# Attention output projection: from fp32 products to three rounded passes, split into a left half among the units and a right half behind them, with GpSimd making the low parts

## The chip, the cores and the metric

The kernel runs on one core of a Trainium2 chip. The metric is device time in microseconds for one inference step, the median of three runs: 1342.69 us (1341.06 to 1346.56). Smaller is better. The profile is one execution taken by the hardware profiler; its times are in microseconds from the first instruction.

## What is computed

Two layers over 512 prompt rows and 32 sample rows of width 1024. Layer 0 mixes tokens by pooling, layer 1 by band attention with 16 heads of 64; each is followed by a mixture of experts (32 experts, each row uses two) whose weights, 6 MB an expert, are read from HBM. The change is in layer 1, between the attention and the router:

```python
o = band_attention(q, band(k), band(v), qpos, kpos, rel_bias)   # softmax(q k / 8 + bias) v
y = jnp.einsum('bse,ed->bsd', o.reshape(B, S, D), w_o)          # the output projection, 1024 x 1024
...
xp = xp + yp                                                   # residual
xp = xp + hier_moe(rms_norm(xp, norm_ffn[i]), *moe_args)        # router, then experts
```

## The kernel before

Instructions are written out per engine, in a fixed order, with semaphores between them; there is no scheduler. The rows are held in four prompt tiles of 128 rows (0 to 3) and one of 32 sample rows.

**Units.** Attention runs as 36 units: for each prompt tile, from tile 3 down to tile 0, eight units of two heads (`PAIRS` = 8; 512, 384, 256 and 128 keys for tiles 3, 2, 1, 0), then four units for the sample rows. `t` counts them. `LONG_UNITS` = 16 are those of tiles 3 and 2. Each engine walks the same loop over `t`, one step behind the other:

- TensorE: `scores(t)` (L2353), transposes of the weights of unit t-2 (L2377), `values(t-3)` (L2393), then, in some steps, four products of the output projection (L2443).
- VectorE: `biased(t)` adds the bias (L1770), `scaled(t-1)` divides by the sum (a reciprocal L1779 and two tensor_scalar L1782), `pT_out(t-2)` copies the second head's transposed weights (L1790).
- ScalarE: `weights(t)` is the exponential (L1253), `pT_out(t-2)` copies the first head's transposed weights (L1264). After four units `oT_out` (L1277) copies the attention's output, transposed, to `oT`.
- GpSimd: `load_bias(u)` issues the load of unit u's bias (L882), once VectorE is done with unit u-5; `hide_later_chunk(u-1)` (L889) waits for the landing of the one before and masks a corner.

**The output projection** of a tile is 16 products (8 row blocks `k` of `w_o` times two column halves `hf`), each a 128x128 by 128x512 matmul in fp32, accumulated in one PSUM bank (`WO_BANK`). `products_at(t)` puts four of them, as one chunk, behind every second unit from t = 12 to 34, and behind each of t = 35 to 38 (tile 0). When a half is whole, VectorE adds it to the residual (`add_product`, L1798), and ScalarE squares a finished row early (`early_squares`, L1289). So rows of tiles 3, 2 and 1 are normalised and stored while the last units still run. The sample's projection (`sample_product`, L2421; 16 products of 32 columns, four side by side on TensorE, and a `fold`, L2428) comes behind the loop, and then `route(1)`: transposes (L1864), router logits (L1930), top-1 and top-2 on VectorE, and the first gather of rows.

**Three rounded passes** are in the kernel already, for the q, k, v projection: an operand is split into a rounded high part and the rest, both in fp32r, and `split_product` forms high·high + low·high + high·low:

```python
mm(out, x_hi, w_h, start=start, stop=False)
mm(out, x_lo, w_h, start=False, stop=False)
return mm(out, x_hi, w_l, start=False, stop=stop)
```

**Weight loads.** SyncE issues the experts' weights (gate, up and down, 2 MB each) into three sets of buffers. Those of the first three experts of layer 1 go into memory that the attention still uses, so each waits for its piece to come free: down of expert 1 and 2 and gate of expert 0 during the units, up and down of expert 0 when all attention output is out, gate and up of expert 1 when the sample's projection is done, gate of expert 2 at the router's logits, and up of expert 2 after the first gather (L621). Behind it the loads of expert 3 follow, freed piece by piece by the first expert's matmuls (L665).

## Time and profile before

| | before |
|---|---|
| median of 3 runs (lowest, highest) | 1342.69 us (1341.06, 1346.56) |
| profiled execution, first to last instruction | 1340.0 us; its own time is not listed apart, the median is 2.7 us above this span |
| TensorE busy | 1291.8 us (96%) |
| VectorE, ScalarE, GpSimd busy | 574.1, 304.7, 127.9 us |
| bytes moved | 459.65 MB, 343 GB/s over the span |
| attention units of layer 1 | from 700 to 840 us |
| router of layer 1 | from 840 to 875 us |
| experts of layer 1 | from 875 us to the end |

A row of instructions gives start, duration, engine, line, operation, output and inputs, and how often it comes in the merged row; in square brackets is how long the engine had been idle, and whose signal ended that. PE is TensorE's matmul, PEld its weight load, DVE VectorE, ACT ScalarE, POOL GpSimd, SPq SyncE's DMA queue. One fp32 matmul of the program stands as two MATMUL rows or counts.

### The profile page before, as it was taken

The page shows a single profiled execution, that of the slowest core. Times are in us where ns is not written, and L with a number is a line of the kernel's source. Part 1 is how long each engine was busy: PE and PEld are TensorE (multiplying, and loading weights), DVE is VectorE, ACT ScalarE, POOL GpSimd, SP SyncE. Part 2 cuts the span into 40 slices and gives each one's busy share as a digit, 9 for nine tenths or more (in the row PEclk, how much of TensorE's full clock was granted, in tenths as well). Part 3 has the DMA queues.
Part 4 walks back from the last instruction along what each step waited for, and adds up shares of the span by engine and source line. Part 5 has one row for each costly group of instructions (what it writes and reads, how often), then busy time and mean ns, then how long its engine had stood idle before and what let it go on. Part 6 is the DMA issues. An engine that isn't in the chain of part 4 may idle for free.

```text
span 1340.0 us, 19743 instructions
## 1 busy us (share of the span) xinstructions
PE 1291.8 (96%) x7448; PEld 638.2 (48%) x7448; DVE 574.1 (43%) x1062; ACT 304.7 (23%) x650; POOL 127.9 (10%) x205
## 2 busy tenths in 40 slices
PE   8899999999999999999999999899999999999998
PEld 6643344333343334788777544443444334343333
DVE  4543334433333433864419543543334334343433
ACT  4211111111111113443436432211111111111111
POOL 2010000000000000232233210000000000000000
PEclk9989999999999999999999999899999999999999
DMA  9989999999999999222058512999999999999996
GB/s 360 380 334 420 424 428 426 427 429 427 428 427 427 428 425 402 69 93 97 34 174 273 181 33 78 380 344 420 426 427 426 427 428 428 427 428 427 426 426 255
DMA packets 53569, 459.65 MB, mean 343 GB/s; under 512 B 8141, under 2 KB 9421, under 8 KB 28170
## 3 DMA queue, kind: packets, MB, share of 16 engines
q1 hardware_dynamic: 41246, 426.48, 76.5%
q0 software_dynamic: 9616, 23.95, 5.5%
q10 hardware_dynamic: 2652, 8.45, 1.7%
q8 instruction: 39, 0.64, 0.2%
q14 instruction: 16, 0.13, 0.0%
HBM read 455.44 MB, written 11.26 MB: 348 GB/s over the span
## 4 chain that ended last, share of the span: by engine, by line
PE 91%; issue 3%; DVE 3%; ACT 2%; DMA 1%; POOL 0%; SPq 0%; DVEq 0%; ACTq 0%; POOLq 0%
PE ps L2014 34%; PE ps L2045 11%; PE ps L2023 9%; PE ps L2024 8%; PE ps L2443 4%; PE ps L1843 3%; PE ps L1845 3%; PE ps L1844 3%; PE ps L2006 2%; PE ps L2377 1%; PE ps L2393 1%; PE ps L1916 1%; PE ps L2032 1%; PE ps L2353 1%; PE ps L1864 1%
## 5 line engine op out<-in xcount | busy, mean ns | idle before, releaser
L1592 DVE TENSOR_TENSOR x<-x,ps 128x1024 f32<-128x1024 f32 (+1 forms) x150 | 177.7, 1216 | 220.9 <-PE ps L2045 219.8
L1606 DVE SCALAR_TENSOR_TENSOR nat<-nat,slot_gate,ps 64x256 f32<-64x256 f32 x128 | 86.1, 672 | 196.3 <-ACT nat L1093 164.7
L2014 PE MATMUL ps<-pair,xT 128*64 128x512 f32 x352 | 163.8, 616 | 6.1 <-issue 6.1
L2014 PE MATMUL ps<-ring,xT 128*64 128x512 f32 x352 | 160.9, 606 | 8.0 <-issue 6.4
L2015 PE MATMUL ps<-pair,xT 128*64 128x512 f32 x352 | 164.0, 616 | 0.0
L2045 PE MATMUL ps<-y_parts,hot 64*128 64x512 f32 (+1 forms) x1200 | 161.3, 403 | 0.0
L2015 PE MATMUL ps<-ring,xT 128*64 128x512 f32 x352 | 161.1, 607 | 0.0
L2014 PE MATMUL ps<-third_pair,xT 128*64 128x512 f32 x320 | 143.6, 596 | 6.9 <-issue 6.9
L1093 ACT ACTIVATE nat<-ps 64x512 f32<-64x512 f32 x62 | 36.8, 594 | 485.5 <-PE ps L2015 485.5
L2024 PE MATMUL ps<-qk,hidT 128*64 128x512 f32 x320 | 144.9, 595 | 0.0
L2023 PE MATMUL ps<-qk,hidT 128*64 128x512 f32 x320 | 144.8, 595 | 0.0
L2015 PE MATMUL ps<-third_pair,xT 128*64 128x512 f32 x320 | 143.8, 597 | 0.0
L2045 PEld LDWEIGHTS ps<-y_parts,hot 64*128 64x128 f32 (+1 forms) x1200 | 98.9, 171 | 72.3 <-issue 48.7
L1569 DVE TENSOR_TENSOR y_parts<-ps,y_parts 128x512 fp32r<-128x512 f32 x60 | 41.5, 692 | 132.5 <-ACT y_parts L1078 132.5
L2014 PEld LDWEIGHTS ps<-pair,xT 128*64 128x64 f32 x352 | 46.9, 140 | 97.2 <-issue 96.0
L2014 PEld LDWEIGHTS ps<-ring,xT 128*64 128x64 f32 x352 | 46.3, 139 | 96.5 <-issue 95.5
L2014 PEld LDWEIGHTS ps<-third_pair,xT 128*64 128x64 f32 x320 | 41.4, 137 | 85.8 <-issue 84.7
L2023 PE MATMUL ps<-ring,hidT 128*64 128x512 f32 x176 | 79.6, 595 | 1.6 <-ACT xT L1059 1.6
L2024 PE MATMUL ps<-ring,hidT 128*64 128x512 f32 x176 | 79.7, 596 | 0.0
L1078 ACT ACTIVATE y_parts<-ps 128x512 fp32r<-128x512 f32 x60 | 35.8, 597 | 192.4 <-PE ps L2024 192.4
L1843 PE MATMUL ps<-w_hi,hT_hi 128*128 128x512 f32 x192 | 76.8, 400 | 0.7 <-DVE hT_lo L1374 0.7
L769 POOL DMA_INDIRECT nat<-xn,gcol x30 | 30.7, 1022 | 467.9 <-PE ps L2006 428.8
(261 smaller groups left out, 1780.3 us busy)
## 6 DMA issues: line engine op xcount, KB each, us to landing
qk<-in_moe_w_down SPq DMA_DIRECT2D x40, 2048.0 KB, 28.5
ring<-in_moe_w_down SPq DMA_DIRECT2D x22, 2048.0 KB
ring<-in_moe_w_gate SPq DMA_DIRECT2D x20, 2048.0 KB, 23.7
ring<-in_moe_w_up SPq DMA_DIRECT2D x20, 2048.0 KB
third_pair<-in_moe_w_gate SPq DMA_DIRECT2D x20, 2048.0 KB, 22.7
third_pair<-in_moe_w_up SPq DMA_DIRECT2D x20, 2048.0 KB
pair<-in_moe_w_gate SPq DMA_DIRECT2D x18, 2048.0 KB
pair<-in_moe_w_up SPq DMA_DIRECT2D x18, 2048.0 KB, 29.7
```

Source lines behind the costliest of these rows:

```text
L1569: V.tensor_tensor(y_rest[v], ps[:, bank, :], f32(y_high[v]), ALU.subtract).then_inc(y_lo[l], 1)
L1592: return V.tensor_tensor(x[0:n, i, :], x[0:n, i, :], ps[0:n, bank:bank + 2, :].rearrange("p b c -> p (b c)"), ALU.add)
L1606: last = V.scalar_tensor_tensor(out=out[u * BLK:(u + 1) * BLK, :].rearrange("s (k p) -> s k p", k=n), in0=act_rows[:, u * n:(u + 1) * n, : ...
L1843: mm(out, x_hi, w_h, start=start, stop=False)
L1844: mm(out, x_lo, w_h, start=False, stop=False)
L1845: return mm(out, x_hi, w_l, start=False, stop=stop)
L2014: mm(ps[BLK:P, GU_BANK, :], rows, gate[:, at], start=(k == 0), stop=(k == KT - 1))
L2015: last = mm(ps[0:BLK, GU_BANK, :], rows, up[:, at], start=(k == 0), stop=(k == KT - 1))
L2023: mm(ps[0:BLK, bank, :], rows, slot[:, at:at + 512], start=(k == 0), stop=(k == FT - 1))
L2024: last = mm(ps[BLK:P, bank, :], rows, slot[:, at + 512:at + D], start=(k == 0), stop=(k == FT - 1))
L2045: last = mm(ps[0:n, bank + hf, :], (hot[v] if by is None else by)[slots, tok(i)], part[slots, :], start=first and at == 0, stop=final and ...
L2443: last = mm(ps[:, WO_BANK, :], oT[:, k, tok(i)], wo_all[:, k, hf * 512:(hf + 1) * 512], start=(k == 0), stop=(k == KT - 1))
```

## The change

The output projection is done with `split_product` on rounded parts. The 16 blocks of `w_o` (c = 0 to 15; 8 of the left half, 8 of the right) are loaded apart, 256 KB each: the first eight into `pair`, the others into places of `nat` and `qk` as tiles finish. ScalarE rounds the high part of each block (`wo_rounded`) and of each group of attention output (`oT_rounded`); GpSimd subtracts to make the low parts (`wo_rest`, `oT_rest`, 25 tensor_tensor instructions on 128x512 elements, the last on 128x256) between its bias loads. The left half of tiles 3, 2 and 1 runs one product behind each of t = 15 to 22 and 25 to 32 and two behind each of t = 34 to 37. Behind the loop stand tile 0's left half, the sample's left half, and then the whole right half. Squares, scaling and stores of the finished rows move behind the loop. From unit 16 on VectorE no longer copies transposed weights: one ScalarE instruction copies both heads' (`pT_both`). The load of down for expert 1 moves behind the projection.

```diff
+        PRODUCTS = {**{15 + k: [(TILES - 1, k)] for k in range(KT)}, **{25 + k: [(TILES - 2, k)] for k in range(KT)},
+                    **{34 + k // 2: [(TILES - 3, k - 1), (TILES - 3, k)] for k in range(1, KT, 2)}}
+        ADDED_AT = {max(t for t, at in PRODUCTS.items() if at[0][0] == i): i for i in range(1, TILES)}
+        WO_SPLIT = {**{6 + c: c for c in range(8)}, **{21 + c - 8: c for c in range(8, 14)}, 31: 14, 38: 15}
...
             def pT_out(t):
+                elif t < PROMPT_UNITS:
+
+                    act.wait_ge(pT_ps, heads_through(t))
+                    act.activation(pT_both[t % 2][:, :, 0:n], ps[:, PT_BANK:PT_BANK + 2, 0:n], ACT.Copy).then_inc(pT_first, 1)
...
+            def wo_rounded(c):
+
+                s, count = wo_landed(c)
+                act.wait_ge(piece_in[s], count)
+                act.activation(wo_part(c, 1), wo_raw(c), ACT.Copy).then_inc(split_hi, 1)
...
+            def wo_rest(c):
+
+                pool.wait_ge(split_hi, QKV_QUARTERS + c + 1)
+                last_own(split_lo, QKV_QUARTERS + c + 1)
+                pool.tensor_tensor(wo_part(c, 0), wo_raw(c), f32(wo_part(c, 1)),
+                                   ALU.subtract).then_inc(split_lo, 1)
...
             for u in range(BIASES, PAIRS * TILES):
                 load_bias(u)
                 if u > BIASES:
                     hide_later_chunk(u - 1)
+                rests(u - BIASES)
...
-            def tile_product(i, first, n):
...
-                    last = mm(ps[:, WO_BANK, :], oT[:, k, tok(i)], wo_all[:, k, hf * 512:(hf + 1) * 512],
-                              start=(k == 0), stop=(k == KT - 1))
...
+            def part_product(hf, i, k):
+
+                c = hf * KT + k
+                pe.wait_ge(split_lo, QKV_QUARTERS + c + 1)
+                return split_product(ps[:, WO_BANKS[hf][i], :], oT_hi[:, k, tok(i)], oT_lo[:, i, k, :],
+                                     wo_part(c, 1), wo_part(c, 0), k == 0, k == KT - 1)
...
-                if products_at(t) is not None:
-                    tile_product(*products_at(t))
+                for i, k in PRODUCTS.get(t, []):
+                    if k == 0:
+                        pe.wait_ge(oT_lo_sb, GROUPS_OUT * (TILES - i) // TILES)
+                        if i < TILES - 1:
+                            pe.wait_ge(x_half, turn(3, i))
+                    last = part_product(0, i, k)
+                    if k == KT - 1:
+                        last.then_inc(att_y, 1)
+
+            pe.wait_ge(oT_lo_sb, GROUPS_OUT)
+            for k in range(KT):
+                last = part_product(0, 0, k)
+            last.then_inc(att_y, 1)
+            pe.wait_ge(oT_lo_sb, GROUPS_OUT + 1)
+            for k in range(KT):
+                last = sample_product(0, k)
+            last.then_inc(quarters_used, 1)
+            for i in range(TILES - 1, -1, -1):
+                if i == 0:
+                    pe.wait_ge(x_half, TILES)
+                    for k in range(KT):
+                        last = sample_product(1, k)
+                    last.then_inc(stack_ps, 1)
+                for k in range(KT):
+                    last = part_product(1, i, k)
+                last.then_inc(att_y, 1)
             transposes(3, TILES - 1)
-            for hf in range(2):
-                sample_product(hf)
             route(1)
```

How TensorE's row of instructions looks among the units of tile 0 (128 keys), before: two units, and a chunk of four products ahead of them and behind them. L2443 is a product, L2353 scores, L2377 transposes, L2393 values.

```order
L2443 MATMUL ps<-pair,third_pair 128x512 x4
L2353 MATMUL ps<-qk 128x128 x2
L2377 MATMUL ps<-cst,gain 128x128 x2
L2393 MATMUL ps<-ring,nat 64x128 x2
L2353 MATMUL ps<-qk 128x128 x2
L2377 MATMUL ps<-cst,ring 128x128 x2
L2393 MATMUL ps<-ring,nat 64x128 x2
L2443 MATMUL ps<-pair,third_pair 128x512 x4
```

The same place now, where scores are L2475, transposes L2499, values L2515 and a product's three passes L1965 to L1967:

```order
L1965 MATMUL ps<-wo_pair,oT_hi 128x512
L1966 MATMUL ps<-wo_pair,oT_lo 128x512
L1967 MATMUL ps<-wo_pair,oT_hi 128x512
L2475 MATMUL ps<-qk 128x128 x2
L2499 MATMUL ps<-cst,ring 128x128 x2
```

One product instead of four, but behind every unit; between two units stand three short matmuls.

GpSimd's queue at units 11 to 14 before: a bias load is issued, and the mask of the one before is set when that has landed (`bias_in`).

```order
L882 DMA ring<-in_rel_bias_reversed 128x2x384 [waits s_biased]
L889 MEMSET ring 64x2x64 [waits bias_in0]
L882 DMA ring<-in_rel_bias_reversed 128x2x384 [waits s_biased]
L889 MEMSET ring 64x2x64 [waits bias_in1]
L882 DMA gain<-in_rel_bias_reversed 128x2x384 [waits s_biased]
L889 MEMSET ring 64x2x64 [waits bias_in2]
```

The same queue now (the load is L935, the mask L951, `wo_rest` L985, `oT_rest` L978):

```order
L951 MEMSET ring 64x2x64 [waits bias_ready,bias_in1]
L985 TENSOR_TENSOR wo_pair<-pair,wo_pair 128x512 [waits bias_ready,split_hi]
L935 DMA gain<-in_rel_bias_reversed 128x2x384 [waits s_biased]
L951 MEMSET ring 64x2x64 [waits split_lo,bias_in2]
L985 TENSOR_TENSOR wo_pair<-pair,wo_pair 128x512 [waits bias_ready,split_hi]
L935 DMA ffn_gain<-in_rel_bias_reversed 128x2x384 [waits s_biased]
L951 MEMSET gain 64x2x64 [waits split_lo,bias_in3]
L978 TENSOR_TENSOR oT_lo<-third_pair,oT_hi 128x512 [waits bias_ready,oT_sb]
L985 TENSOR_TENSOR wo_pair<-pair,wo_pair 128x512 [waits oT_lo_sb,split_hi]
```

A subtraction or two now stand between a mask and the next unit's load. Behind the loop TensorE's queue was, from the last values on:

```order
L2409 MATMUL ps<-ring,nat 64x32 x2
L2443 MATMUL ps<-pair,third_pair 128x512 x4
L1864 MATMUL ps<-cst,x 128x128 x8
L2421 MATMUL ps<-pair,third_pair 32x512 x16
L1864 MATMUL ps<-cst,x 128x128 x8
L2428 MATMUL ps<-gain,cst 32x512 x2
L1864 MATMUL ps<-cst,x 128x128 x16
L1930 MATMUL ps<-third_pair,rw 64x384 x8
```

Now 24 passes for tile 0's left half, 16 for the sample's (L2549 to L2552), 72 for the right half of tiles 3, 2 and 1, 16 more for the sample and 24 for tile 0 stand there, and then:

```order
L1967 MATMUL ps<-wo_nat,oT_hi 128x512
L1986 MATMUL ps<-cst,x 128x128 x16
L2557 MATMUL ps<-gain,cst 32x512 x2
L1986 MATMUL ps<-cst,x 128x128 x16
L2052 MATMUL ps<-third_pair,rw 64x384 x8
```

The transposes, the fold and the router's logits keep their order; 40 products, 24 of them of tiles 3 to 1, have moved in front of them from the loop.

## Rows read from the trace of the kernel before

**Rows 1.** Windows: busy us and (count) per engine, granted clock, DMA share, GB/s.

```profile
core 0: us, PE busy (x) PEld busy (x) DVE busy (x) ACT busy (x) POOL busy (x), PEclk, DMA share, GB/s
...
782.00:837.00 55.00, 53.02 (x331) 26.83 (x330) 20.63 (x100) 19.24 (x74) 3.88 (x9) 1.00 0.19 58
...
850.00:875.00 25.00, 21.01 (x90) 11.68 (x90) 15.99 (x55) 4.48 (x11) 1.98 (x2) 0.80 0.83 339
...
900.00:1150.00 250.00, 249.59 (x1450) 101.31 (x1448) 98.94 (x135) 36.45 (x73) 10.80 (x18) 1.00 1.01 426
1150.00:1300.00 150.00, 140.61 (x794) 57.15 (x792) 54.88 (x75) 19.77 (x40) 4.80 (x8) 0.98 1.01 427
```

**Rows 2.** SyncE's DMA queue, timeline around the start of layer 1's experts.

```profile
872.35 0.33 SPq L621 DMA_DIRECT2D third_pair<-in_moe_w_up  x1
877.02 0.33 SPq L665 DMA_DIRECT2D ring<-in_moe_w_gate  x1
```

**Rows 3.** The chain that ended last, from the last chunk to the logits: start, us, what.

```profile
836.67 3.63 PE ps L2443 x8
...
841.19 3.62 PE ps L2421 x32
...
847.77 0.69 DVE x L1798
848.48 1.16 ACT xT L928 x2
...
850.49 2.80 PE ps L1930 x16
```

**Rows 4.** TensorE, timeline: a chunk of four products, and what starts behind it.

```profile
761.94 3.70 PE L2443 MATMUL ps<-pair,third_pair 128*128 128x512 f32 x8
765.57 0.70 PE L2353 MATMUL ps<-qk 64*128 64x256 f32 x4
...
836.60 3.70 PE L2443 MATMUL ps<-pair,third_pair 128*128 128x512 f32 x8
...
840.13 1.05 PE L1864 MATMUL ps<-cst,x 128*128 128x128 f32 x8
```

**Rows 5.** TensorE, timeline in the q, k, v projection: three rounded passes.

```profile
689.63 0.39 PE L1843 MATMUL ps<-w_hi,hT_hi 128*128 128x512 f32 x1
...
690.31 0.39 PE L1843 MATMUL ps<-w_hi,hT_hi 128*128 128x512 f32 x1
```

**Rows 6.** TensorE, groups by line in 733 to 837 us: busy, mean ns, idle before.

```profile
L2377 PE MATMUL ps<-cst,ring 128*128 128x128 f32 x76 | 12.8, 285 | 3.4 <-ACT ring L1264 2.4 <-DVE ring L1790 0.9
```

**Rows 7.** Timeline of unit 11: VectorE's work, and TensorE's transposes that wait.

```profile
732.40 0.56 DVE L1770 CUSTOM_DVE_ANT_0 ring<-ps,ring 128x384 f32<-128x384 f32 x1 [0.31 <-issue]
...
733.56 0.75 DVE L1782 TENSOR_SCALAR ring<-ring 128x384 f32<-128x384 f32 x2
734.23 0.55 DVE L1790 COPY ring<-ps 128x384 f32<-128x384 f32 x1
734.87 0.56 DVE L1770 CUSTOM_DVE_ANT_0 ring<-ps,ring 128x384 f32<-128x384 f32 x1
...
734.88 0.30 PE L2377 MATMUL ps<-cst,ring 128*128 128x128 f32 x1 [0.15 <-ACT ring L1264]
```

**Rows 8.** A line's instructions: duration ns min/median/max, first and last start, forms.

```profile
L860 POOL TENSOR_TENSOR nat<-nat,qk_gain x20: 1275/1298/2278, 560.5 to 657.6; 128x512 f32<-128x512 f32 x16, 32x512 f32<-32x512 f32 x4
...
L1361 DVE TENSOR_TENSOR w_lo<-ring,w_hi x24: 1210/1226/2307, 534.3 to 677.3; 128x1024 fp32r<-128x1024 f32 x24
```

**Rows 9.** Timeline around 562 us: a subtraction on VectorE beside a product on GpSimd.

```profile
561.75 2.28 POOL L860 TENSOR_TENSOR nat<-nat,qk_gain 128x512 f32<-128x512 f32 x1
...
562.80 2.31 DVE L1361 TENSOR_TENSOR w_lo<-ring,w_hi 128x1024 fp32r<-128x1024 f32 x1
```

**Rows 10.** Timeline of GpSimd's bias loads and masks, and VectorE's scaling beside one.

```profile
722.80 0.72 POOL L882 DMA_DIRECT2D ring<-in_rel_bias_reversed  x1
...
724.82 0.91 DVE L1782 TENSOR_SCALAR ring<-ring 128x512 f32<-128x512 f32 x2
...
725.11 0.33 POOL L889 MEMSET ring<- 64x128 f32 x1 [1.60 <-DMA ring<-in_rel_bias_reversed]
...
727.30 0.20 POOL L889 MEMSET ring<- 64x128 f32 x1 [1.21 <-DMA ring<-in_rel_bias_reversed]
```

More of the change, by code:

```diff
@@ L290, in encoder, with wo_part, wo_raw @@
         rw_experts = xT_flat[:, KT * NG:KT * NR].rearrange("p (g n) -> p g n", g=NG)
+        pair_flat = pair[:, :, :].rearrange("p a n -> p (a n)")
+        def wo_part(c, part):
+            where, u = WO_PLACES[c]
+            return wo_parts[where][:, u, part, :]
+        def wo_raw(c):
+            where, u = WO_PLACES[c]
+            flat = (pair_flat, nat[:, :], qk_flat[:, SLOT:])[where]
+            return flat[:, u * 1024:u * 1024 + 512]
         early_rows = third_pair[:, 1, :]
@@ L305, in encoder @@
                  for u in range(2)]
+        pT_both = [a4[:, 2 * D + u * 1024:2 * D + (u + 1) * 1024].rearrange("p (h n) -> p h n", h=2) for u in range(2)]
         BIASES_RING, BIASES = 3, 5
@@ L910, in _ @@
                     hide_later_chunk(u - 1)
+                rests(u - BIASES)
             hide_later_chunk(PAIRS * TILES - 1)
+            for t in range(PAIRS * TILES - BIASES, UNITS + 4):
+                rests(t)
+            oT_rest(GROUPS_OUT)
             experts(1)
@@ L1013, in logitsT_out @@
                 act.wait_ge(logitsT_ps, 2 * l + part + 1)
-                cols = part_cols(part)
+                cols = part_cols(part) if part == 0 else slice(part_cols(part).start, NT * P)
                 act.activation(logitsT[:, cols], ps[:, LOGITST_BANKS[l][part], 0:cols.stop - cols.start],
@@ L1292, in _ @@
             for t in range(UNITS + 4):
-                if t >= 4 and t - 4 < PROMPT_UNITS and (t - 4) % OT_GROUP == OT_GROUP - 1:
-                    oT_out(t - 4)
+                if group_at(t, OT_GROUP + 3) is not None:
+                    oT_out(group_at(t, OT_GROUP + 3))
                 if t < UNITS:
@@ L1300, in _ @@
                     pT_out(t - 2)
-                for i, hf in halves_before(t - 1):
-                    if hf == 1 and i > 0:
-                        early_squares(i)
+                if group_at(t, OT_GROUP + 4) is not None:
+                    oT_rounded(group_at(t, OT_GROUP + 4))
+                if t in WO_SPLIT:
+                    wo_rounded(WO_SPLIT[t])
                 if t == UNITS:
                     load_sqrt_table()
-                    act.wait_ge(act_own, own[0])
-                    act.activation(std[:, 3, 1:TILES], ssq[:, 3, 1:TILES], ACT.Sqrt, bias=const("eps"),
-                                   scale=1.0 / D).then_inc(std_ready, TILES - 1)
-            oT_out(UNITS - 1)
+            oT_out(GROUPS_OUT)
+            oT_rounded(GROUPS_OUT)
             for i in range(TILES - 1, 0, -1):
+                early_squares(i)
+            act.wait_ge(act_own, own[0])
+            act.activation(std[:, 3, 1:TILES], ssq[:, 3, 1:TILES], ACT.Sqrt, bias=const("eps"),
+                           scale=1.0 / D).then_inc(std_ready, TILES - 1)
+            for hf in range(2):
+                wo_stack_out(hf)
+            for i in range(TILES - 1, 1, -1):
                 store_row(1, i)
@@ L2411, in values @@
                 last.then_inc(o_ps, 1)
-            def sample_product(hf):
-                if hf == 0:
-                    pe.wait_ge(oT_sb, OT_ALL)
-                    pe.wait_ge(x_mixed[1], TILES)
-                half = slice(hf * 512, (hf + 1) * 512)
-                for k in range(KT):
-                    at = k % HEADS_A_GROUP * SS
-                    last = mm(ps[at:at + SS, WO_SAMPLE_BANKS[hf], :], oT[:, k, S:T], wo_all[:, k, half],
-                              start=(k < HEADS_A_GROUP), stop=(k >= KT - HEADS_A_GROUP))
-                last.then_inc(stack_ps, 1)
+            def part_product(hf, i, k):
[3 more added lines that the diff above has]
+                                     wo_part(c, 1), wo_part(c, 0), k == 0, k == KT - 1)
@@ L2425, in sample_fold @@
             def sample_fold(hf):
                 pe.wait_ge(stack_sb, 2 * QKV_PIECES + hf + 1)
[L2428 removed]
+                mm(ps[0:SS, WO_SAMPLE_BANKS[hf], :], const("fold", 2 * SS), wo_stacked[hf], start=True,
                    stop=True).then_inc(att_y, 1)
[L2431 to L2446 removed]
```

214 lines of the change are left out of this document (136 added, 78 removed).

## The prediction

> **What bounds the kernel now.** I read the windows by stage first. From 900 us to the end of the experts the DMA engines are busy all the time at 426 to 427 GB/s [rows 1], while in the attention (782 to 837 us) their share is 0.19 and in the router it is 0.83. So the experts' stage is a stream of fixed length, and what counts is when it starts. It starts where the first experts' buffers, all filled ahead, begin to come free: SyncE's queue issues the last of the nine early loads at 872.35, and expert 3's first piece at 877.02, when the first expert's matmuls free it [rows 2]. Both hang on the router. Loads that the change delays (down of expert 1, gate and up of expert 1) land long before that, in a stage whose DMA is mostly idle; they cost nothing as long as 2 MB at that rate, 5 us, fit between the end of the projection and the first gather, some 30 us later.
>
> Then the chain of waits, from the attention to the router. It is on TensorE: the last chunk, the sample's products, then short steps on VectorE and ScalarE, and the logits at 850.49 [rows 3]. TensorE is busy for 53.02 of 55 us in the last units [rows 1]; its own waits for the pipeline from 733 to 837 us are 3.4 us before the transposes of the weights [rows 6]. So up to the logits the time is TensorE's queue, and an edit is worth what it takes out of it or makes it wait. From the logits on the program is as before; I carry a shift there through to the end.
>
> **The sum.** I count up to the end of the last values (836.6) and from there to the logits.
>
> *Removed before 836.6.* A chunk of four fp32 products moves what follows by 765.57 - 761.94 = 3.63 us [rows 4]. Fifteen of the sixteen lie there (t = 12 to 34 by twos, 35, 36, 37): 54.5 us.
>
> *Added before 836.6.* Three rounded passes take 690.31 - 689.63 = 0.68 us, 0.227 each [rows 5], against 0.91 for a product of a chunk. But a chunk has a cost of its own when the next matmul is of another shape. In the chunk at 836.60 the same eight matmuls take 3.53 us [rows 4], so that 0.10 depends on the neighbour; the rows of a chunk are some 0.43 apart, 3.42 in all, by which the cost is 0.1 to 0.2. I take 0.21, since the new chunks stand between values and scores as that of 761.94 does. Sixteen chunks of one product make 16 x 0.89 = 14.2 us, four of two make 4 x 1.57 = 6.3, together 20.5.
>
> *Behind 836.6.* Before, the logits come 13.9 us later: 3.5 for the last chunk, 3.6 for the sample [rows 3], and 6.8 for transposes, fold, two additions, a square of the sample's rows and a copy. Now 40 products (27.2) and 32 passes for the sample (7.3) come first, 34.5 us, and the same 6.8 behind them: 41.3. The additions, squares and scalings of tiles 3 and 2 lie beside the 34.5 us; of tile 1, one scaling on VectorE comes behind the last product, beside TensorE's transposes and fold. Net 27.4 us more.
>
> These three give 54.5 - 20.5 - 27.4 = 6.6 us less.
>
> *The pipeline's waits.* The chunks of 3.63 us behind every second unit let VectorE and ScalarE run ahead. With 0.89 behind every unit, TensorE still has more to do in a unit than the round trip takes in most units; units 23, 24, 32 and 33 have no product and will wait some tenths each. VectorE gains its copy (0.55 us [rows 7]) in units 16 to 31, ScalarE gets some 0.5 us a unit more and was busy for only 19.24 of 55 us [rows 1]. Bounds: 1.4 and 6 us against 3.4 before. I take 2.4, so 1.0 less.
>
> *GpSimd's subtractions.* No such instruction stands in the attention now; the nearest row is the product of 128x512 on GpSimd, 1.29 us undisturbed and up to 2.28 [rows 8]. Two that meet say why [rows 9]: while GpSimd runs, VectorE's subtraction of two SBUF operands goes from 1.23 to 2.31, and GpSimd's from 1.29 to 2.28; each waits for the other's whole instruction. What stands beside them in the attention is VectorE's tensor_scalar, with one SBUF operand. The only row for it is the mask of 725.11, which took 0.33 instead of 0.20 beside a tensor_scalar of 724.82, while that was not slowed [rows 10]: they do meet, by 0.13 at least. Upper bound: a full block. In units 7 to 15 VectorE is busy for 2.38 of 2.47 us and TensorE's transposes start right when its copy ends [rows 7], so there a delay of VectorE is one of TensorE. A subtraction that starts at any time in 2.47 us holds up the first of the two tensor_scalars for 0.65 us on average in 1.29/2.47 of the cases, and comes between the two, for the whole 1.29, in 0.34/2.47 (0.34 being about half of their 0.75): 0.51 us, less 0.09 of slack. Ten subtractions fall there (blocks 0 to 7, groups 0 and 1): 4.2 us. Thirteen come in later units, where VectorE has 0.8 us to spare without its copy: 0.1 each, 1.3. So between 0 and 5.5; I take 3.0, the middle, as the row nearest in place shows a part of the block and the row nearest in kind all of it.
>
> *Low parts that come late.* GpSimd waits for a bias to land, 4.5 us after its issue (722.80 to 727.30 [rows 10]), before each mask; with a subtraction of 1.29 behind the mask a step takes (4.5 + 0.2 + 1.3)/2 = 3.0 us instead of 2.47, over eight units some 4 us of lag. The masks are made four units ahead and stay in time. The low part of tile 3 is made two units, 5 us, ahead of its first product, behind such a lag: 0 to 2 us late; by then TensorE has lost some of the same time, so 0.5. Queued behind GpSimd's waits are only its own masks; behind TensorE's wait are all scores that follow.
>
> Sum: -6.6 - 1.0 + 3.0 + 0.5 = -4.1. The span goes from 1340.0 to 1335.9, and with the 2.7 us between span and median the time is **1338.6 us**. With its own bounds that case reaches from 1336 to 1341.
>
> **The rule on the shared port.** The rows above show full blocking for two SBUF operands, and a small one for a tensor_scalar. The Trainium skill says in "SBUF — State Buffer", section "Who interferes with whom", that tensor_scalar can run in a mode that takes the port pair VectorE shares with GpSimd, and that the later of the two then "fully blocks" until the first is done. By that the block of 5.5 us above holds in full, the low parts come later too (1.0), and the sum is -6.6 - 1.0 + 6.5 = -1.1: 1341.6. No row here shows it for a tensor_scalar beside a GpSimd instruction that reads. That speaks against this change, and has a chance of its own below.
>
> **Rivals.**
> *GpSimd costs little.* If a tensor_scalar isn't held up and the low parts are in time, the sum is -7.6, and with chunks that cost 0.10 like that of 836.60 instead of 0.21 another 20 x 0.1 = 2.0 less: -9.6, 1333.1. For it: tensor_scalar of 724.82 kept its 0.91 beside the mask. Against: the full blocking of [rows 9].
> *Full block:* 1341.6, worked out above.
> *The two engines lock into step.* Low parts start when masks end, not at random; if each of the 23 subtractions comes just ahead of or between the tensor_scalars, each costs up to 1.29 less the slack: 10 x 1.20 + 13 x 0.49 = 18.4. Then -7.6 + 18.4 + 0.5 = +11.3, 1354.0, slower. It decides from 14.3 us of GpSimd's cost on (that gives +6.7). Against it: bias landings vary from step to step.
> *It is hidden behind DMA.* If the weight stream, not the router, set the restart, nothing would move: 1342.7. For it: the share of 1.01 [rows 1]. Against: at 850 to 875 us the share is 0.83, and expert 3's first load waits for matmuls, not for room in the queue.
>
> **Chances and range.** The forecast's case 0.37, GpSimd costs little 0.31, full block 0.15, locked into step 0.10, hidden 0.07. A measurement of this kernel can tell 0.5% (6.7 us, below 1336.0 or above 1349.4) from no change. Faster: all of the second case and a sixth of the first, 0.37. Slower: the step-lock and a few hundredths of the unforeseen, 0.13. Within: 0.50. The range reaches from the cheap case, 1332, to beyond the full block, 1346; it leaves out the step-lock and the low end of the second case, about 2 in 10.
>
> **What would show it right or wrong.** In the profile after: passes 0.227 us apart among the units and behind them; the logits some 41 us behind the last values, and at about 846.4 instead of 850.5; last values near 805 instead of 836.6; GpSimd's subtractions at 1.3 us, or up to 2.3 where they meet; VectorE's tensor_scalar longer than its 0.75 for two in units 7 to 15, which decides between the cases; TensorE's waits before the transposes at 2 to 9 us; the wait for the low part before the first product of tile 3 under 2 us; the DMA share still 1.01 from 900 us on. The prediction is wrong if the logits' shift isn't the end's, if ScalarE's rounding delays the exponentials (TensorE would wait for ScalarE's copies in each unit), or if the clock that is granted in the router (0.80 from 850 to 875 us [rows 1]) falls otherwise.

## The result: 0.3% slower, and the profile after

The changed kernel takes 1348.52 us (median of 20 executions, 1341.04 to 1354.26); the kernel before took 1343.76 beside it. The ratio is 1.0031, with a 95% interval from 1.0015 to 1.0046; one execution of the kernel before took 1626.41 us and is left out of it. That is some 4 us slower, where 4 us less were forecast, and outside the range. The profiled execution of the changed kernel spans 1344.3 us, 4.3 more than that of before.

Windows of the changed kernel (columns as in [rows 1]):

```profile
core 0: us, PE busy (x) PEld busy (x) DVE busy (x) ACT busy (x) POOL busy (x), PEclk, DMA share, GB/s
782.00:837.00 55.00, 52.07 (x345) 36.61 (x344) 13.22 (x60) 18.99 (x60) 13.99 (x15) 0.94 0.57 216
850.00:875.00 25.00, 22.11 (x101) 12.88 (x101) 15.30 (x47) 7.24 (x16) 1.39 (x2) 0.80 0.58 207
900.00:1150.00 250.00, 249.04 (x1450) 101.47 (x1448) 97.84 (x135) 37.03 (x75) 10.83 (x18) 1.00 1.01 426
```

The experts' stage is the same stream at 426 GB/s, and the router has the clock of before, 0.80. What is new is the 0.94 from 782 to 837 us, where before had 1.00.

TensorE, timeline: the first scores, a wait before the transposes of a unit, the last values, the logits.

```profile
703.06 2.00 PE L2475 MATMUL ps<-qk 64*128 64x256 f32 x16
...
737.91 0.85 PE L2499 MATMUL ps<-cst,ring 128*128 128x128 f32 x6 [1.44 <-issue]
...
813.27 0.30 PE L2531 MATMUL ps<-ring,nat 32*64 32x32 f32 x4
...
854.78 2.80 PE L2052 MATMUL ps<-third_pair,rw 128*64 128x384 f32 x16 [0.79 <-ACT third_pair L1092]
```

Before, the logits began at 850.49 [rows 3] and the span ended 489.5 us later; here it is 854.78 and again 489.5. So in these two profiles the shift of the logits is that of the end, and all of it arises before them. (Over all fourteen profiles that last part takes 488.3 to 492.6 us.) The attention itself began 3.1 us later (703.06; before 699.92), with the same instructions ahead of it; a control below shows what that is worth. To be rid of it I compare the stretch from the first scores to the logits: 150.6 us before, 151.7 now, forecast 146.5 (150.6 less 4.1).

From the last values to the logits it is 41.2 us (854.78 - 813.57), as forecast (41.3; before 13.9). The loss lies among the units: 110.5 us from the first scores to the last values, forecast 105.2. TensorE's waits there, 700 to 815 us:

```profile
PE ps L2499 <- issue: 4.7, 6, 1.4
PE ps L2515 <- ACT third_pair L1375: 2.7, 1, 2.7
```

The first line is the one that I had priced: units 7 to 15, where VectorE is late. The profile names no releaser for it; experiment 2 shows that these waits go with GpSimd's subtractions. The second is one wait that no step of mine had. Around it, ScalarE:

```profile
783.94 0.63 ACT L1391 ACTIVATE wo_nat<-nat 128x512 fp32r<-128x512 f32 x1 [2.52 <-DMA nat<-in_attn_w_o]
784.48 0.58 ACT L1375 ACTIVATE third_pair<-ps 128x512 f32<-128x512 f32 x1
```

SyncE's queue:

```profile
760.74 0.33 SPq L665 DMA_DIRECT2D nat<-in_attn_w_o  x1
...
780.79 0.33 SPq L665 DMA_DIRECT2D nat<-in_attn_w_o  x1
```

And TensorE:

```profile
785.20 0.70 PE L2515 MATMUL ps<-ring,nat 128*64 128x128 f32 x4 [2.69 <-ACT third_pair L1375]
...
788.75 0.70 PE L2515 MATMUL ps<-ring,nat 128*64 128x128 f32 x4
...
792.06 0.44 PE L2515 MATMUL ps<-ring,nat 128*64 128x128 f32 x4
792.43 0.50 PE L1965 MATMUL ps<-wo_pair,oT_hi 128*128 128x512 f32 x1
```

At unit 26's step ScalarE rounds block 13 of `w_o`. That block was issued at 760.74, but ScalarE waits until 783.94. The reason is in the code: `WO_LOADS` counts the landings of blocks 13 and 14 together, on one semaphore, and block 14 is issued only when tile 1's place in `nat` is free, at 780.79, in that same step. Behind the rounding stands `oT_out`, and for that TensorE's values wait 2.69 us. Then TensorE goes on slowly: a unit's step takes 3.55 us from 785.20 to 788.75. The windows of 2 us say why:

```profile
782.00:784.00 2.00, 0.50 (x4) 0.27 (x2) 1.19 (x8) 0.06 (x1) 1.03 (x3) 1.00 0.51 170
...
786.00:788.00 2.00, 2.00 (x7) 1.17 (x7) 0.00 (x0) 0.09 (x1) 1.80 (x4) 0.50 0.11 25
788.00:790.00 2.00, 2.00 (x10) 1.11 (x9) 1.07 (x7) 1.31 (x6) 0.88 (x2) 0.50 0.28 49
...
792.00:794.00 2.00, 2.00 (x15) 1.18 (x13) 1.01 (x8) 1.15 (x5) 0.70 (x1) 1.00 0.20 49
```

A granted clock of 0.50 is 1.2 GHz in place of 2.4. TensorE stood idle, and right behind it the clock was at half until shortly before 792.

### The profile page after: what moved, and what is told of

Read it like the earlier page. It is cut to its first block, busy times and chain, and to the rows that moved or that the text cites. A ratio compares the mean times of both kernels' runs of the same rounds, so it can differ in the third digit from the quotient of the medians.

```text
span 1344.3 us, 19958 instructions
## 1 busy us (share of the span) xinstructions
PE 1289.9 (96%) x7512; PEld 655.1 (49%) x7512; DVE 577.8 (43%) x1046; ACT 321.0 (24%) x675; POOL 158.7 (12%) x230
## 4 chain that ended last, share of the span: by engine, by line
PE 92%; issue 3%; DVE 2%; ACT 1%; DMA 1%; POOL 0%; SPq 0%; POOLq 0%; DVEq 0%; ACTq 0%
PE ps L2136 34%; PE ps L2167 11%; PE ps L2145 9%; PE ps L2146 8%; PE ps L1965 5%; PE ps L1967 4%; PE ps L1966 4%; PE ps L2128 2%; PE ps L2515 2%; PE ps L2499 2%; PE ps L2475 1%; PE ps L2038 1%; PE ps L2154 1%; PE ps L1961 1%; PE ps L2374 1%
## 5 line engine op out<-in xcount | busy, mean ns | idle before, releaser
L2136 PE MATMUL ps<-ring,xT 128*64 128x512 f32 x352 | 162.8, 612 | 9.8 <-issue 8.2
L2136 PE MATMUL ps<-pair,xT 128*64 128x512 f32 x352 | 160.6, 606 | 5.8 <-issue 5.8
L2137 PE MATMUL ps<-ring,xT 128*64 128x512 f32 x352 | 163.0, 613 | 0.0
L2137 PE MATMUL ps<-pair,xT 128*64 128x512 f32 x352 | 160.8, 607 | 0.0
L2136 PE MATMUL ps<-third_pair,xT 128*64 128x512 f32 x320 | 145.0, 601 | 6.7 <-issue 6.7
L2146 PE MATMUL ps<-qk,hidT 128*64 128x512 f32 x320 | 144.9, 595 | 0.0
L1965 PE MATMUL ps<-w_hi,hT_hi 128*128 128x512 f32 x192 | 77.4, 403 | 0.7 <-DVE hT_lo L1493 0.7
```

What stands on the lines that cost most here:

```text
L2136: mm(ps[BLK:P, GU_BANK, :], rows, gate[:, at], start=(k == 0), stop=(k == KT - 1))
L2137: last = mm(ps[0:BLK, GU_BANK, :], rows, up[:, at], start=(k == 0), stop=(k == KT - 1))
L2146: last = mm(ps[BLK:P, bank, :], rows, slot[:, at + 512:at + D], start=(k == 0), stop=(k == FT - 1))
```

## The experiments

**0. Control: the kernel before again.**

> The kernel before once more, as a control. In the profile after, the attention began at 703.06 us instead of 699.92, with the same instructions in front of it; 1.5 us of that come from layer 0 and 1.6 from a short fall of the granted clock near 560 us. Theory A (that offset of 3.1 us is chance and not the change's): this kernel's profile begins the attention anywhere in 699 to 704 us, its executions lie within some 1340 to 1349 us, with a mean granted clock of 0.983 to 0.987 in all of them. Theory B (the changed kernel is slower because TensorE's clock falls more often in it): the same for this kernel, but with a visibly narrower spread of the clock than the 0.975 to 0.986 of the changed one. If this kernel's executions show 0.975 to 0.980 too, B is out.

Measured: ratio 1.0017 (0.9999 to 1.0035); executions from 1341.62 to 1351.16 us, mean clock 0.980 to 0.988, both a little wider than I had allowed. Its profile has the first scores at 705.98, also later than allowed, and the stretch to the logits is 150.8 us, 0.2 more than in [rows 3]. The first scores of all fourteen profiles of this study lie between 699.7 and 706.0: the offset of 3.1 us is chance, and the stretch is what can be compared. Theory B isn't out: none of these 12 executions, and none of the 35 of the kernel before beside them, has a mean clock below 0.980, while 8 of the changed kernel's 20 have (0.975 to 0.979), and these 8 took 1348 us or more. The medians are 0.985 and 0.980.

**1. Block 13's landing counted alone.** One line of the changed kernel:

```diff
-        WO_LOADS = [(0, range(0, 4)), (1, range(4, 8)), (2, range(8, 13)), (0, range(13, 15)), (1, range(15, 16))]
+        WO_LOADS = [(0, range(0, 4)), (1, range(4, 8)), (2, range(8, 13)), (0, range(13, 14)), (1, range(14, 15)), (0, range(15, 16))]
```

> The changed kernel with one edit: the landing of block 13 of w_o is counted apart from that of block 14 (which is issued only at unit 26's step, just when ScalarE rounds block 13). Theory A: the wait of 2.52 us in front of ScalarE's rounding of block 13 is gone, with it TensorE's wait of 2.69 us before the values at 785, and the half clock that followed it (some 2 us): 4.7 us less than the changed kernel, 1343.8 against 1348.5. Theory B (the clock falls because of the many short waits in units 7 to 15): only the 2.7 us go, 1345.8, and the executions still spread over some 12 us with clocks down to 0.975.

Measured: 1337.66 us, ratio 0.9966 (0.9945 to 0.9987); median clock 0.987.

```profile
704.27 2.00 PE L2475 MATMUL ps<-qk 64*128 64x256 f32 x16
...
782.18 0.44 PE L2515 MATMUL ps<-ring,nat 128*64 128x128 f32 x4
...
784.25 0.44 PE L2515 MATMUL ps<-ring,nat 128*64 128x128 f32 x4
...
849.78 2.80 PE L2052 MATMUL ps<-third_pair,rw 128*64 128x384 f32 x16 [0.79 <-ACT third_pair L1092]
```

The wait is gone and a step takes 2.07 us. The stretch is 145.5 us, 6.2 less than in the changed kernel: the wait of 2.7, the half clock (two steps of 3.4 on average in place of 2.05, 2.7 in all), and 0.8 of other waits. The median fell by more than the 4.7 us that I expected, by 10.9 (8.7 by the ratios). So this one pair of counts makes a slower kernel out of a faster one. Theory B had the short waits of units 7 to 15 bring on the fall; they are still here, and the clock is 1.00 from 700 to 840 us. The executions do still spread over 10 us. That the median gains more than the profile shows fits the clock, by an estimate: 0.980 and 0.987 differ by 0.007 x 1345 = 9.4 us of full clock, more than the one fall of the profiled execution. Where the rest of it lies no profile shows.

**2. Ten subtractions cut to a sixteenth.**

```diff
+                    m = slice(0, 8) if g < 2 else slice(0, P)
+                    pool.tensor_tensor(oT_lo[:, i, at, m], oT_raw[:, i, at, m], f32(oT_hi[:, at, tok(i)])[:, :, m],
...
+                m = slice(0, 32) if c < 8 else slice(0, 512)
+                pool.tensor_tensor(wo_part(c, 0)[:, m], wo_raw(c)[:, m], f32(wo_part(c, 1))[:, m],
...
```

> The changed kernel with ten of GpSimd's subtractions (w_o blocks 0 to 7 and tile 3's two groups, all in units 7 to 15) cut to a sixteenth of their elements; the products read the high part in place of those low parts, so the output is not the reference's but every matmul is issued. Theory A (VectorE's tensor_scalar waits for the whole GpSimd instruction): the pairs of tensor_scalar that took 0.83 to 2.64 us go back to 0.75 to 0.8, TensorE's waits between 733 and 752 (4.4 us) go, 1344.1. Rival (the units are late because of the bias loads and masks behind GpSimd's longer queue, or ScalarE's added rounding): the tensor_scalars shorten but TensorE gains under 1.5 us, 1347. The wait at block 13 stays in both.

Measured: 1346.21 us, ratio 1.0026 (1.0006 to 1.0046), which by the time alone can't be told from the changed kernel's 1.0031. In the profile Theory A holds. TensorE's waits up to the last values fell from 9.3 to 4.5 us, but the stretch only from 151.7 to 150.2, since the clock stayed low longer behind the wait for block 14:

```profile
778.00:780.00 2.00, 2.00 (x9) 1.07 (x7) 0.00 (x0) 0.45 (x3) 1.81 (x4) 0.50 0.00 0
780.00:790.00 10.00, 10.00 (x39) 5.54 (x39) 3.32 (x21) 4.44 (x17) 3.78 (x4) 0.50 0.21 66
```

Some 13 us at half clock here, some 7 in the changed kernel's profile, behind the same wait of 2.7. The waits of units 7 to 15 don't bring the fall on: they are gone here, and the fall is not. Six of these 12 executions have a mean clock below 0.980.

**5. The wait filled with work.** In front of the values that wait in the changed kernel:

```diff
+                        if t == 24:
+                            for _ in range(6):
+                                mm(ps[:, S_BANK, 256:512], ident, some[:, 0:256], start=True, stop=True,
+                                   skip_group_check=True)
                         pe.wait_ge(oT_sb, 2 * (t // OT_GROUP) - 1)
```

> The changed kernel (block 13 still counted with block 14), with six matmuls of 128x256 on the identity, some 2.7 us of work, put in front of the values for which TensorE waits 2.69 us. The wait stays as long, but the engine is busy in it. Theory C (what costs most is not the wait but the half clock that the wait brings on behind it: 6.8 us of half clock in the changed kernel's profile, 13.6 in that of e2): the granted clock stays 1.00 from 780 to 800 us, 4 to 7 us less than the changed kernel (1348.5), so 1342 to 1344.5, and 3 to 4 us above e1. Rival (the half clock is brought on by the product chunks or the mix of short matmuls there): as the changed kernel, 1348.5.

Measured: 1341.24 us, ratio 0.9981 (0.9963 to 0.9999), 7.3 us less than the changed kernel by the medians, 6.7 by the ratios; none of the 12 executions has a mean clock below 0.982, and in the profile it is 1.00 from 780 to 800 us. Timeline of TensorE:

```profile
780.02 2.76 PE L2512 MATMUL ps<-cst 128*128 128x256 f32 x12
782.77 0.44 PE L2519 MATMUL ps<-ring,nat 128*64 128x128 f32 x4
```

The values are as late as without the filling, and the steps behind them take 2.05 us. So of the price of that wait one part, 2.4 us in the stretch (147.9 against experiment 1's 145.5), is the wait itself. The other part is the half clock behind it: the stretch is 3.8 us shorter than the changed kernel's, 1.1 of it in other waits, so 2.7, and the median gains more than that. The Trainium skill says in "TensorE: Matmul & The Clock Gate", section "Why this matters for your kernels", that a TensorE left idle between matmuls drops to its lower clock. By the changed kernel and this run that is so at this place. It is not so each time: in the changed kernel's own profile TensorE waits 2.65 and 2.66 us between two experts, with the same work before and behind, and only one of the two waits is followed by a fall.

```profile
1227.53 0.61 PE L2136 MATMUL ps<-pair,xT 128*64 128x512 f32 x1 [2.65 <-issue]
1288.36 0.61 PE L2136 MATMUL ps<-third_pair,xT 128*64 128x512 f32 x1 [2.66 <-issue]
```

The windows of 8 us behind them (the granted clock is the third figure from the end):

```profile
1228.00:1236.00 8.00, 8.00 (x38) 3.18 (x36) 2.35 (x2) 0.00 (x0) 0.00 (x0) 0.79 1.01 428
1289.00:1297.00 8.00, 8.00 (x45) 3.36 (x42) 2.35 (x2) 0.00 (x0) 0.00 (x0) 1.00 1.01 428
```

What decides between them no run here shows.

**6. Small subtractions, with block 13 counted alone** (edits of 1 and 2 together).

> e1 with the ten subtractions of units 7 to 15 cut to a sixteenth as in e2 (their products read the high part instead, so the output is not the reference's). This measures the blocks without the half clock on top. TensorE waited 3.3 us between 725 and 752 us in e1. Theory A: those waits go, from the first scores to the logits 142.5 us instead of 145.5, 1334.7. Rival (VectorE catches up later by itself, since TensorE has other waits to absorb it): under 1 us less than e1.

Measured: 1335.01 us, ratio 0.9948 (0.9934 to 0.9961); the stretch is 142.3 us. This is the price of the ten subtractions, 3.2 us, from one profile of each kernel; the ratios of experiments 1 and 6 overlap in their intervals. The view of a block in the changed kernel, two of VectorE's pairs of tensor_scalar in units 7 to 15:

```profile
734.70 2.64 DVE L1901 TENSOR_SCALAR ring<-ring 128x384 f32<-128x384 f32 x2
...
744.59 0.83 DVE L1901 TENSOR_SCALAR ring<-ring 128x384 f32<-128x384 f32 x2
```

GpSimd beside the first of them:

```profile
734.44 1.27 POOL L978 TENSOR_TENSOR oT_lo<-third_pair,oT_hi 128x512 fp32r<-128x512 f32 x1
735.86 1.26 POOL L985 TENSOR_TENSOR wo_pair<-pair,wo_pair 128x512 fp32r<-128x512 f32 x1
```

And VectorE in experiment 6:

```profile
733.97 0.75 DVE L1903 TENSOR_SCALAR ring<-ring 128x384 f32<-128x384 f32 x2
```

The pair that met two subtractions lost 1.89 us; GpSimd's instructions never took over 1.32. This is the full block of the rule in the Trainium skill, "SBUF — State Buffer", section "Who interferes with whom", seen here for a tensor_scalar: VectorE's instruction stands until GpSimd's has ended.

**3, 4 and 8. The splitting of `w_o` moved to where VectorE has room.**

```diff
-        WO_SPLIT = {**{6 + c: c for c in range(8)}, **{21 + c - 8: c for c in range(8, 14)}, 31: 14, 38: 15}
+        WO_SPLIT = {**{16 + c: c for c in range(14)}, 31: 14, 38: 15}
```

with the products later by some steps, as each expectation says, and in 4 and 8 in GpSimd's loop:

```diff
                 load_bias(u)
-                if u > BIASES:
-                    hide_later_chunk(u - 1)
                 rests(u - BIASES)
+                if u > BIASES + 1:
+                    hide_later_chunk(u - 2)
```

> e1's edit, and the splitting of w_o moved as a whole to steps 16 to 29, where VectorE no longer copies transposed weights; the left-half products follow (tile 3 at 19 to 26, tile 2 at 27 to 34, tile 1 two by two at 35 to 38). Nothing is left out. Theory A: the blocks cost next to nothing there (two tensor_scalars of 256 or 128 columns take 0.62 of a unit in which VectorE idles 0.7 to 1.2 us), the two groups of tile 3 still cost some 1 us: 3.4 us less than e1, 1340.4. Rival (there is no slack there either, TensorE loses 0.5 us for each block): as e1, 1343.8. Rival (low parts come late for the first products, three steps behind their splitting): slower than e1 by 2 us or more, with TensorE waiting for POOL.

> e3 with its own trouble mended: in e3 a mask on GpSimd waited 5.3 us for a bias load that shared the DMA queues with 2 MB of the gate weights, the low part of a w_o block stood behind it, and TensorE waited 4.3 us in front of a product. Here each mask is set one step later and the subtraction stands ahead of it, and tile 3's products follow at steps 20 to 27, tile 2's at 28 to 35, tile 1's by three, three and two at 36 to 38. Theory A (VectorE's tensor_scalar waits for GpSimd only where the unit has no slack): from the first scores to the logits 142.5 us (e1 145.5, e3 149.8), so 3 us less than e1, 1334.7. Rival (the blocks cost the same wherever they are): as e1, 1337.7. Rival (a low part is late again): over 1340, with a wait for POOL in TensorE's list.

> e4 lost 3.4 us in one wait at 782: tile 2's first product stood one step behind tile 3's last, in the same PSUM bank, and VectorE's addition that empties it was queued behind the next unit's work. Here one step lies between them (tile 3 at steps 19 to 26, tile 2 at 28 to 33, tile 1 at 35 to 38); masks later and late splits as in e4; and on ScalarE the copy of tile 1's last transposes goes ahead of the square of the sample's rows (0.8 us before the logits). Theory A: e4's 148.2 us from the first scores to the logits, less 3.4, less 1.7 of half clock, less 0.8: 142.3, three below e1's 145.5, 1334.5. Rival (late splits always trade the blocks for another wait): 145 or more, as e1 or slower.

Measured: 3 has 1343.08 us (ratio 1.0004, 0.9983 to 1.0025), a stretch of 149.8; 4 has 1344.4 (1.0007, 0.9993 to 1.0021), 148.2; 8 has 1338.04 (0.9963, 0.9942 to 0.9985), 144.9. In each the blocks of units 7 to 15 are gone (but for those of tile 3's two groups), and in each another wait has come. GpSimd's timeline in 3: the mask stands until the bias has landed, behind 2 MB of gate weights, and the subtraction behind the mask.

```profile
762.99 0.20 POOL L951 MEMSET gain<- 64x128 f32 x1 [5.26 <-DMA gain<-in_rel_bias_reversed]
763.34 1.26 POOL L985 TENSOR_TENSOR wo_pair<-pair,wo_pair 128x512 fp32r<-128x512 f32 x1
```

TensorE's in 3, then in 4:

```profile
764.65 0.76 PE L1965 MATMUL ps<-wo_pair,oT_hi 128*128 128x512 f32 x1 [4.33 <-POOL wo_pair L985]
```

```profile
782.34 0.47 PE L1966 MATMUL ps<-wo_pair,oT_hi 128*128 128x512 f32 x1 [3.37 <-issue]
```

The wait in 3 is the second rival of its expectation. The wait in 4 has two causes in a row. I placed tile 2 directly behind tile 3, in the bank that VectorE had yet to empty. And VectorE, whose addition empties it, was itself late: it had stood 2.95 us for a mask, which GpSimd set only behind two subtractions, in the order that this experiment's own edit made.

```profile
780.53 0.29 DVE L1890 CUSTOM_DVE_ANT_0 ring<-ps,gain 128x128 f32<-128x128 f32 x1 [2.95 <-POOL gain L951]
...
781.56 0.68 DVE L1918 TENSOR_TENSOR x<-x,ps 128x512 f32<-128x512 f32 x1
```

Behind both the granted clock was 0.83 over ten microseconds, where neighbours had 1.00. In 8 no wait is over 1.2 us, but they sum to 5.6 us as in experiment 1: 3 us of blocks were traded for waits on ScalarE (2.9 us), VectorE (1.2) and low parts (0.8). The rival of experiment 8 held: its stretch is experiment 1's within 0.6 us.

**7. Each tile product one fp32 matmul, in place.**

```diff
-                return split_product(ps[:, WO_BANKS[hf][i], :], oT_hi[:, k, tok(i)], oT_lo[:, i, k, :],
-                                     wo_part(c, 1), wo_part(c, 0), k == 0, k == KT - 1)
+                return mm(ps[:, WO_BANKS[hf][i], :], f32(oT_hi[:, k, tok(i)]), f32(wo_part(c, 1)),
+                          start=(k == 0), stop=(k == KT - 1))
```

> e1 with every product of the four prompt tiles as one fp32 matmul on the rounded high parts (low parts are made but not read by them, so the output is not the reference's); order, splitting, waits and the sample's product are e1's. This tells what the three passes give by themselves. By my sum a product costs 0.91 instead of 0.68 us: 64 x 0.23 = 14.7 us more than e1 from the first scores to the logits, 160.2 us, and 1352.4. Rival (in the units TensorE waits for VectorE in any case, so that 20 products among them hide a part of it): 10 to 12 us more, 1348 to 1350.

Measured: 1347.89 us, ratio 1.0042 (1.0026 to 1.0057), a stretch of 156.6, 11.1 us more than experiment 1. Nothing of it is hidden: behind the last values the 40 products take 7.1 us more, 0.18 each, and the 24 among the units 4.0, 0.17 each. So an fp32 product costs 0.68 + 0.18 = 0.86 us, which is what the forecast's chunk of 3.63 gives less its 0.21; my expectation of 14.7 had counted the chunk's own cost with each product. The 11.1 us lie in the rival's range, but its reason, that waits among the units hide a part, did not hold.

**9. The copies apart.**

```diff
-                if t < LONG_UNITS:
+                if t < PROMPT_UNITS:
                     act.wait_ge(pT_ps, heads_through(t - 1) + 1)
...
-                if 0 <= t - 2 < LONG_UNITS:
+                if 0 <= t - 2 < PROMPT_UNITS:
                     pT_out(t - 2)
...
```

> e1 with the third part of the change undone: in units 16 to 31 VectorE copies the second head's transposed weights again, ScalarE only the first's. By my sum VectorE's 0.5 us a unit there was worth 1.0 us of TensorE's waits together with everything else, so 0 to 2 us more than e1: 145.5 to 147.5 from the first scores to the logits. Rival (without that relief the pipeline is bound by VectorE in every unit, as in units 7 to 15): 16 x 0.3 = 5 us more, 150, with waits for VectorE's copy in each unit.

Measured: 1340.49 us, ratio 0.997 (0.9953 to 0.9987); stretch 147.3, 1.8 more than experiment 1. TensorE's waits for the pipeline are 7.5 in place of 5.6 us. So this part of the change is worth some 2 us by the profiles, within what I had expected; by the ratios experiments 1 and 9 are the same.

**10. Products in pairs behind every second unit.**

```diff
-        PRODUCTS = {**{15 + k: [(TILES - 1, k)] for k in range(KT)}, **{25 + k: [(TILES - 2, k)] for k in range(KT)},
+        PRODUCTS = {**{15 + k: [(TILES - 1, k), (TILES - 1, k + 1)] for k in range(0, KT, 2)},
+                    **{25 + k: [(TILES - 2, k), (TILES - 2, k + 1)] for k in range(0, KT, 2)},
```

> e1 with the products of tiles 3 and 2 two by two behind every second unit (steps 15, 17, 19, 21 and 25, 27, 29, 31) instead of one behind each. My sum gives each chunk 0.21 us of its own: 8 fewer chunks, 1.7 us less than e1, 143.8 us from the first scores to the logits, 1336. Rival (the cover that a chunk gives VectorE and ScalarE is then missing behind every other unit, and TensorE waits there): same as e1 or up to 2 us more.

Measured: 1342.25 us, ratio 0.999 (0.9974 to 1.0006); stretch 149.6, 4.1 more than experiment 1, beyond my rival. TensorE's waits, 700 to 815 us:

```profile
PE ps L2500 <- issue: 2.9, 5, 1.2
PE ps L2500 <- ACT ring L1360: 2.6, 7, 0.5
PE ps L2500 <- DVE ring L1910: 2.6, 2, 1.7
PE ps L2500 <- DVE ring L1902: 1.4, 3, 0.8
PE ps L2516 <- ACT third_pair L1376: 1.1, 2, 0.7
```

They are 10.6 us in place of 5.6. The product behind every unit is worth more as cover for the other engines than eight chunks of 0.21 cost.

**11. Subtractions in halves, and a swap on ScalarE.**

```diff
+                for part in (slice(0, 256), slice(256, 512)):
+                    last = pool.tensor_tensor(wo_part(c, 0)[:, part], wo_raw(c)[:, part], f32(wo_part(c, 1))[:, part],
...
+            first_chunks(1, TILES - 3)
             row_squares(1, NT - 1)
-            first_chunks(1, TILES - 3)
```

> e1 with every subtraction of GpSimd on a 128x512 block as two of 128x256 behind each other, and on ScalarE the copy of tile 1's last transposes ahead of the square of the sample's rows (0.8 us before the logits). Theory A (a tensor_scalar that meets a subtraction waits until that one instruction ends, and can start before the next): the longest pairs of tensor_scalar fall from 2.6 to about 1.5 us, the blocks of 3 us that e6 measured (145.5 against 142.3) fall to about a half, and with the swap the stretch from the first scores to the logits is 143.2 us, 1335.4. Rival (GpSimd takes the port again before VectorE can, or each half costs as much as the whole through its own start): 144.7, only the 0.8 us of the swap, or a little more than e1.

Measured: 1337.74 us, ratio 0.9969 (0.9948 to 0.9989); stretch 145.0, so 0.5 less than experiment 1. The swap gave 0.8 us between the last values and the logits (40.4 in place of 41.2, with no wait before the logits). The halves gave nothing: up to the last values it is 104.5 us, where experiment 1 has 104.3. The rival held. GpSimd's row and VectorE's near 737 us:

```profile
737.00 1.69 POOL L988 TENSOR_TENSOR wo_pair<-pair,wo_pair 128x256 fp32r<-128x256 f32 x2
```

```profile
736.88 1.23 DVE L1905 TENSOR_SCALAR ring<-ring 128x384 f32<-128x384 f32 x2
```

A pair of halves takes 1.41 to 1.69 us where the whole took 1.27, and almost every pair of tensor_scalar is now long (0.99 to 1.78) where some had been at 0.83. The blocks became shorter and more frequent. Over seven pairs they sum to 3.6 us, and to 3.6 in experiment 5 too, where the subtractions are whole. In the changed kernel, whose instructions are the same as experiment 5's up to 780 us, it is 5.6: so much varies from one execution to the next.

## Why the prediction was wrong, point by point

**The chunks and what stands behind them: right.** Forecast were 34.0 us out, 27.4 in. The part behind the last values came out at 41.2 us of 41.3. Experiments 1 and 6 have 104.3 and 101.1 us from the first scores to the last values, where before had 136.7. Less TensorE's waits (5.6, 1.6 and 4.5) that is 98.7, 99.5 and 132.2: 33.5 and 32.7 us out.

**The pipeline's waits: right in sign, too small.** I took 1.0 off 3.4. Without the blocks (experiment 6) TensorE waits 1.6 us from 700 to the last values, where before it waited 4.5, so 2.9 less; experiment 9 puts 1.8 us down to the joint copy, measured with the blocks in place.

**GpSimd's subtractions: the number near, the mechanism the rival's.** Forecast were 3.0 between 0 and 5.5, a middle between a full block and almost none. The runs show the full block. Experiment 6 measures 3.2 us in the kernel of experiment 1, and for the ten subtractions of units 7 to 15 alone, for which the full block had been priced at 4.2; the other thirteen, priced at 1.3, no run takes out. That the middle came out so near is in part luck. In the changed kernel's own profile the seven pairs of tensor_scalar from 731 to 751 us are 5.6 us longer than 0.75 each (the full block's 0.51 for each of ten makes 5.1), and TensorE waits 4.4 for them from 733 to 750 us; how much of a block reaches TensorE differs from profile to profile.

**Low parts late: nothing** in the changed kernel; 0.5 was forecast. It came true only where I moved the splitting (experiment 3).

**The sum.** -4.1 gives 146.5 us for the stretch and 1338.6 for the kernel. Experiment 1, the changed kernel without one wait, has 145.5 and 1337.66; by its ratio it is 4.6 us below the kernel before. So the sum came out within 1 us but for the term that it lacked, though two of its terms, the pipeline's waits and the late low parts, were too high by some 2 us and 0.5.

**The step that failed** is the sentence that ScalarE "gets some 0.5 us a unit more and was busy for only 19.24 of 55 us". It prices `wo_rounded` by its duration and puts at nothing that the instruction waits for a DMA. In its place the runs showed a wait of 2.52 us on ScalarE, one of 2.69 us on TensorE behind it, and the half clock behind that. I followed the loads that the change delays to the experts, but not the 16 that it adds to those who wait for them: for each, the semaphore, the value, and the step at which the last load in that value is issued. For block 13 that gives the issue of block 14 in the very step in which ScalarE waits, and behind the rounding in ScalarE's queue stood the output copy on which TensorE's values hang. I had named ScalarE's rounding among what could prove me wrong, but with no price and no place in the range.

**Its price** I would have had wrong as well. A DMA's 3.15 us (780.79 to 783.94), less a little slack, is 2.7 us of wait. What followed, the half clock, is 2.7 us in the profiled execution and more in the median: 7.3 us (6.7 by the ratios) between the changed kernel and experiment 5, in which only the idleness is taken away. The fall fits the changed kernel's executions up to 1354 us, since its lowest mean clocks go with its longest times, but no profile was taken of such an execution. How long the fall lasts there I can only tell from the mean clock.

## What to carry to other kernels

When a change adds a wait on a DMA, write down for each waiter which landings its count contains, and where the last of them is issued; loads that share a count are as late as the latest. A single wait of 2 to 4 us on a busy TensorE has a price beyond its length when the clock falls behind it, and the runs bound that price but give no fixed factor: 2.7 us of wait lost 2.7 more in the changed kernel's profile and some 6.7 more in experiment 2's (13.4 us at half clock), 4.3 and 3.4 us lost 1.7 more in experiments 3 and 4 (0.83 over ten), and some waits of 2.7 lost nothing more. The short waits of units 7 to 15 brought on no fall here. And where several engines pass a unit from hand to hand, taking away one engine's delay is worth it only if no other wait is queued up right behind: three rearrangements here won back the 3 us of the blocks; one kept 0.6 of it, the other two lost more than they had won.

## What the hardware showed that I had not expected

- Behind a wait of 2.69 us TensorE's granted clock was 0.50 for some 7 us in one profile and 13 in another, with the engine busy all that time. With six matmuls in the wait it stayed at 1.00. Behind equal waits of 2.65 and 2.66 us between experts, in one and the same profile, it fell once and once not.
- A tensor_scalar with one SBUF operand waits for a whole GpSimd subtraction: a pair of 0.75 us took up to 2.64. Two halves blocked no less than one whole (3.6 us over seven pairs in experiments 11 and 5).
- A bias load of 256 KB that was issued just behind 2 MB of weights landed 8.3 us after its issue (754.67 to 762.99 in experiment 3), where one of 384 KB took 4.5 in [rows 10]. In the changed kernel one of 128 KB, issued at 763.44 behind the same load, took 8.2.
- The Trainium skill, "DMA: Bandwidth & Descriptors", section "Why a DMA increments its semaphore by 16 and not by 1", says that when two loads in flight share a semaphore, a wait for the first one's count can pass before that load has fully landed, and asks for a semaphore for each. No run here shows a count that passed early. The kernel had avoided that by one count over both loads, and paid with the wait of 2.69 us; experiment 1 gives each its semaphore.
